# Branch and output projections of a hybrid decoder layer as three fp32r products of high and low parts

## What is computed

```python
o_a = nsa_attention(...)        # (1024, 512)
o_b = stick_breaking(...)       # (1024, 256)
o_c = swa_with_sinks(...)       # (1024, 256)
g = jax.nn.sigmoid(merge).reshape(B, S, 3, D)
y = g[:, :, 0] * (o_a @ w_branch_a) + g[:, :, 1] * (o_b @ w_branch_b) + g[:, :, 2] * (o_c @ w_branch_c)
return y @ w_out
...
x = x + g_a * hybrid_mixer(...)
h = rmsnorm(x, g_norm_moe[l]) * (1.0 + sc_m) + sh_m
x = x + g_m * grouped_moe(h, ...)
```

## Time and profile before

| | us |
|---|---|
| median of 3 runs | 2056.28 |
| lowest, highest | 2055.0, 2060.48 |
| the profiled execution | 2060.36 |
| its span, first to last instruction | 2058.6 |
| TensorE matmul busy | 1858.1 (90%) |
| DVE busy | 925.8 (45%) |
| ACT busy | 632.7 (31%) |
| mean granted TensorE clock | 0.951 of 2.4 GHz |

### The profile page before, as it was taken

One profiled execution on the slowest core, in us unless ns is written; L12 is line 12 of the kernel. 1 busy time (PEld: TensorE's weight loads), 2 busy tenths in 40 slices (PEclk: granted clock), 3 DMA queues, 4 the chain that ended last, 5 costly groups with the idle time before them and its releaser, 6 DMA issues.

```text
span 2058.6 us, 21698 instructions
## 1 busy us (share of the span) xinstructions
PE 1858.1 (90%) x7869; PEld 1202.3 (58%) x7869; DVE 925.8 (45%) x1505; ACT 632.7 (31%) x1115; POOL 243.7 (12%) x300
## 2 busy tenths in 40 slices
PE   2999999989898989989899888999984999999996
PEld 2554644555455555656556556444554777777875
DVE  5554313233333333334334344453336474759486
ACT  1321101323232323324234234210012353546363
POOL 3211230000000101001011011000001111111211
PEclk9999998999998999999999989999985999999998
DMA  9343321211011001001000040525233587879693
GB/s 341 124 148 119 81 54 25 62 42 42 28 34 33 30 21 36 26 21 36 21 21 16 11 128 6 209 92 214 103 110 84 173 286 200 289 244 348 192 367 94
DMA packets 121391, 232.33 MB, mean 113 GB/s; under 512 B 5832, under 2 KB 44816, under 8 KB 120240
## 3 DMA queue, kind: packets, MB, share of 16 engines
q1 hardware_dynamic: 113312, 203.14, 28.4%
q0 software_dynamic: 7984, 27.93, 6.0%
HBM read 196.44 MB, written 35.65 MB: 113 GB/s over the span
## 4 chain that ended last, share of the span: by engine, by line
PE 74%; DVE 16%; issue 4%; ACT 3%; DMA 1%; ACTq 0%; DVEq 0%; SPq 0%; POOL 0%; POOLq 0%
PE psum L1698 18%; PE psum L1524 9%; DVE arena_r L1403 9%; PE psum L1623 8%; PE psum L1684 7%; PE psum L1734 5%; PE psum L1759 5%; PE psum L1652 4%; PE psum L1544 3%; PE psum L1804 2%; PE psum L1805 2%; PE psum L1809 2%; ACT heads_r L932 1%; DVE negm L1206 1%; DVE kv L989 1%
## 5 line engine op out<-in xcount | busy, mean ns | idle before, releaser
L1698 PE MATMUL psum<-arena 128*128 128x512 f32 x768 | 387.9, 641 | 0.7 <-ACT arena L902 0.4
L1206 DVE TENSOR_REDUCE negm<-psum 128x1 f32<-128x640 f32 (+7 forms) x128 | 90.6, 707 | 431.1 <-PE psum L1625 431.1
L1684 PE MATMUL psum<-kv,arena 128*128 128x64 f32 x1464 | 197.4, 279 | 62.2 <-DVE arena L1190 36.7
L1684 PEld LDWEIGHTS psum<-kv,arena 128*128 128x128 f32 x1464 | 187.6, 200 | 69.9 <-issue 38.2
L1698 PEld LDWEIGHTS psum<-arena 128*128 128x128 f32 x768 | 144.8, 204 | 128.3 <-issue 127.8
L873 ACT ACTIVATE arena<-psum,negm 128x640 f32<-128x640 f32 (+7 forms) x128 | 89.6, 700 | 406.6 <-DVE negm L1206 406.5
L1524 PE MATMUL psum<-arena 128*128 128x512 f32 (+2 forms) x512 | 187.9, 520 | 0.0
L709 POOL TENSOR_SCALAR arena<-arena 128x128 f32<-128x128 f32 (+7 forms) x32 | 76.8, 2401 | 853.7 <-ACT arena L896 853.7
L1804 PE MATMUL psum<-heads_r,kv_r 128*128 128x512 f32 x384 | 151.0, 393 | 13.1 <-DVE kv_r L1409 13.1
L1623 PE MATMUL psum<-kv,heads 112*128 112x512 f32 (+7 forms) x384 | 147.5, 489 | 5.8 <-ACT arena L896 5.2
L1805 PE MATMUL psum<-heads_r,kv_r 128*128 128x512 f32 x384 | 150.8, 393 | 0.0
(11 more groups left out here) (356 smaller groups left out, 2454.7 us busy)
## 6 DMA issues: line engine op xcount, KB each, us to landing
arena<-in_w_exp_gate_dram SPq DMA_DIRECT2D x16, 2048.0 KB
arena<-in_w_exp_up_dram SPq DMA_DIRECT2D x16, 2048.0 KB, 13.1
arena<-in_w_exp_down_dram SPq DMA_DIRECT2D x16, 2048.0 KB, 10.6
arena<-in_w_ada_dram SPq DMA_DIRECT2D x7, 2048.0 KB, 15.2
arena<-in_w_in_dram SPq DMA_DIRECT2D x24, 512.0 KB, 4.1
z_dram<-arena SPq DMA_DIRECT2D x48, 256.0 KB, 2.0
arena<-z_dram SPq DMA_DIRECT2D x8, 1536.0 KB, 6.5
bc<-in_w_ada_dram SPq DMA_DIRECT2D x4, 2048.0 KB, 7.8
```

The source lines that it names most:

```text
L1684: mm = pe.matmul(psum[:, bank, c * HD:(c + 1) * HD], pt[:, j * P:(j + 1) * P], v, start=(j == 0), stop=(j == u["nb"] - 1))
L1698: mm = pe.matmul(GATE_BANK, gate_w[t % 3][:, k, :], hT[:, k, hf * BANK:(hf + 1) * BANK], start=(k == 0), stop=(k == NK - 1))
```

## The change

Both projections are made as the experts' are: high by high, high by low, low by high, in fp32r. The attention result is split in place (`o_hi` in the room of `hT`, `o_lo` over the float32 in `heads`) in the slots from 147 on; branch weights are loaded two groups ahead into a ring of two, and split; both halves of `w_out` are loaded behind z(1), and split in four pieces; `yT` is split tile by tile into rings of two; `x1` becomes a ring of two. The expert weights are loaded in another order. The diff, cut to what matters (index changes of `x1`, `oT` and semaphores left out):

```diff
+        SPLIT0 = FILL0 + 3 * N_GATE + 1
...
         def branch_w(m):
-            a = m % 4 * NK * P
-            return part_of(4 + m // 4, a, a + NK * P)...
+            a = m % 2 * NK * P
+            return part_of(0, a, a + NK * P)...
...
SP
-            for m in range(NK):
+            def load_branch(m):
                 for w, k0, k1 in ((w_branch_a, 0, 4), (w_branch_b, 4, 6), (w_branch_c, 6, 8)):
                     sp.dma_start(branch_w(m)[:, k0:k1, :], w...[:, :, m * P:(m + 1) * P]
-                                 ).then_inc(branch_in[m // 4], 16)
+                                 ).then_inc(branch_in[m % 2], 16)
...
             for i in range(2):
                 sp.wait_ge(z_out[i], 8 * N_GATE)
-            load(L_OUT)
+            load_branch(0)
+            load_branch(1)
...
             load_z(0)
             load_z(1)
-            load(L_OUT + 1)
-            for n in range(2):
-                sp.dma_start(xr[n], x2d[n * P:(n + 1) * P, :]).then_inc(xr_in[n], 16)
+            load_wout(0)
+            load_wout(1)
             for m in range(2, NK):
                 sp.wait_ge(mix_done, 6 * (m - 1))
                 load_z(m)
+                sp.wait_ge(mix_full, 6 * (m - 1))
+                load_branch(m)
...
             sp.wait_ge(mix_done, 3 * 2 * NK)
+            for n in range(2):
+                sp.dma_start(xr[n], x2d[n * P:(n + 1) * P, :]).then_inc(xr_in[n], 16)
+            load_expert(0, 0)
+            load_expert(0, 2)
...
+            sp.wait_ge(out_full, NT)
+            load_expert(0, 1)
             for i in range(3):
                 load_expert(1, i)
-            load_expert(0, 2)
...
POOL
-            pool.wait_ge(x1_out, 16 * NT)
+            for i in range(2):
+                pool.wait_ge(x1_out[i], 8 * NT)
...
ACT
+            def out_hi(n):
+                if n == 0:
+                    act.wait_ge(g_full, N_GATE)
+                for g in out_of[n]["groups"]:
+                    wait_evacuated(act, g)
+                act.activation(o_hi[:, n, :, :], o_raw[:, n, :, :], ACT.Copy).then_inc(o_hi_ok, 1)
+            def branch_weights_hi(m):
+                act.wait_ge(branch_in[m % 2], 16 * 3 * (m // 2 + 1))
+                if m >= 2:
+                    act.wait_ge(mix_full, 6 * (m - 1))
+                act.activation(branch_hi(m), branch_w(m), ACT.Copy).then_inc(bw_hi_ok, 1)
             for q, s in enumerate(slots):
...
+                if 0 <= q - SPLIT0 < NT - 1:
+                    out_hi(q - SPLIT0)
+                elif 0 <= q - SPLIT0 - (NT - 1) < 2:
+                    branch_weights_hi(q - SPLIT0 - (NT - 1))
+            out_hi(NT - 1)
             for m in range(NK):
                 act.wait_ge(z_in[m % 2], 16 * (m // 2 + 1))
                 act.activation(z_group(m), z_group(m), ACT.Sigmoid).then_inc(sig_ok, 1)
+                if m + 2 < NK:
+                    branch_weights_hi(m + 2)
+            act.wait_ge(mix_full, 3 * 2 * NK)
+            act.wait_ge(wout_in[0], wout_n[0])
+            act.activation(wout_chunk(wout_hi, 0), wout_chunk(wout_raw, 0), ACT.Copy).then_inc(wout_hi_ok, 1)
+            act.wait_ge(y_ok, 4 * NK)
             act.wait_ge(mix_done, 3 * 2 * NK)
+            mixed_hi(0)
+            act.wait_ge(wout_in[1], wout_n[1])
+            for c in range(1, 4):
+                act.activation(wout_chunk(wout_hi, c), wout_chunk(wout_raw, c), ACT.Copy).then_inc(wout_hi_ok, 1)
+            mixed_hi(1)
...
                     act.activation(xr[n % 2], x1[n % 2], ACT.Square, accum_out=st[:, SSX:SSX + 1]).then_inc(x1_sq, 1)
+                    if n + 2 < NT:
+                        mixed_hi(n + 2)
...
DVE
+                if 1 <= q - SPLIT0 < NT:
+                    out_lo(q - SPLIT0 - 1)
+                elif 0 <= q - SPLIT0 - NT < 2:
+                    branch_weights_lo(q - SPLIT0 - NT)
+            out_lo(NT - 1)
...
+                if r % 6 == 1 and 1 <= m < NK - 1:
+                    branch_weights_lo(m + 1)
...
             dve.wait_ge(y_ok, 4 * NK)
+            mixed_lo(0)
+            for c in range(4):
+                wout_rest(c)
+            mixed_lo(1)
...
+                    if n >= 2:
+                        dve.wait_ge(x1_out[n % 2], 16 * (n // 2))
...
+                    dve.tensor_tensor(x1[n % 2], x1[n % 2], xr[n % 2], ALU.add).then_inc(x1_ok, 1)
+                    if n + 2 < NT:
+                        mixed_lo(n + 2)
...
PE
-                if r % 24 == 0:
-                    pe.wait_ge(branch_in[m // 4], 16 * 12)
+                if r < 2:
+                    pe.wait_ge(o_hi_ok, 4 * (r + 1))
+                    pe.wait_ge(o_lo_ok, 4 * (r + 1))
+                if r % 6 == 0:
+                    pe.wait_ge(bw_hi_ok, m + 1)
...
                 for k in range(k0, k1):
-                    mm = pe.matmul(psum[:, 2 * (r % 4) + 1, :], branch_w(m)[:, k, :], oT[:, hf * 4:(hf + 1) * 4, k, :], ...)
+                    pe.matmul(bank, branch_hi(m)[:, k, :], o_hi[:, ns, k, :], start=(k == k0), stop=False)
+                    pe.matmul(bank, branch_hi(m)[:, k, :], o_lo[:, ns, k, :], start=False, stop=False)
+                if r % 6 == 0:
+                    pe.wait_ge(bw_lo_ok, m + 1)
+                for k in range(k0, k1):
+                    mm = pe.matmul(bank, branch_lo(m)[:, k, :], o_hi[:, ns, k, :], start=False, stop=(k == k1 - 1))
                 mm.then_inc(mix_full, 1)
...
+                    pe.wait_ge(y_hi_ok, n + 1)
+                    pe.wait_ge(y_lo_ok, n + 1)
```

More of the change, by code:

```diff
@@ L211, in slot_of @@
         def slot_of(i):
-            return HOME[i] if i < L_OUT else i - L_OUT
+            return HOME[i]
         slot_n = [[] for _ in range(5)]
@@ L243, in wait_used @@
                 eng.wait_ge(hid_full, 1)
-            elif i < L_OUT:
+            else:
                 eng.wait_ge(ada_ok, 4 + i - L_ADA2 + 1)
-            else:
-                eng.wait_ge(out_full, NT)
         prob = [tmp[:, i * T:(i + 1) * T] for i in range(2)]
@@ L571, in _ @@
             sp.wait_ge(mix_done, 3 * 2 * NK)
+            for n in range(2):
+                sp.dma_start(xr[n], x2d[n * P:(n + 1) * P, :]).then_inc(xr_in[n], 16)
+            load_expert(0, 0)
+            load_expert(0, 2)
+            for n in range(1, NT + 1):
+                if 2 <= n < NT:
+                    sp.wait_ge(xn2_ok, n - 1)
+                    sp.dma_start(xr[n % 2], x2d[n * P:(n + 1) * P, :]).then_inc(xr_in[n % 2], 16)
+                sp.wait_ge(xn2_ok, n)
+                sp.dma_start(xn_dram[(n - 1) * P:n * P, :], xn2).then_inc(xn2_out, 16)
+                sp.dma_start(out2d[(n - 1) * P:n * P, :], x1[(n - 1) % 2]).then_inc(x1_out[(n - 1) % 2], 16)
+            sp.wait_ge(out_full, NT)
+            load_expert(0, 1)
             for i in range(3):
                 load_expert(1, i)
-            load_expert(0, 2)
[L576 to L591, removed]
             sp.wait_ge(dest_ok, 1)
@@ L916, in _ @@
                         act.wait_ge(x1_rstd, n)
[L917 removed]
+                    act.activation(xr[n % 2], x1[n % 2], ACT.Square, accum_out=st[:, SSX:SSX + 1]).then_inc(x1_sq, 1)
+                    if n + 2 < NT:
+                        mixed_hi(n + 2)
                 if n:
@@ L937, in expert_tokens_hi @@
                                    ACT.Copy).then_inc(xs_hi_ok, 1)
-            act.wait_ge(x1_out, 16 * NT)
+            for i in range(2):
+                act.wait_ge(x1_out[i], 8 * NT)
+            act.wait_ge(xn2_out, 16 * NT)
+            act.wait_ge(y_lo_ok, NT)
             expert_weights_hi(0, None)
@@ L1300, in _ @@
                         dve.wait_ge(mod_rows_act, 1)
-                    own(dve.scalar_tensor_tensor(xn2, x1[:, n, :], stp[:, 1:2], a2_bc, ALU.mult, ALU.mult))
+                    own(dve.scalar_tensor_tensor(xn2, x1[n % 2], stp[:, 1:2], a2_bc, ALU.mult, ALU.mult))
                     dve.tensor_tensor(xn2, xn2, b2_bc, ALU.add).then_inc(xn2_ok, 1)
@@ L1756, in _ @@
                         pe.wait_ge(x1_ok, n - 1)
+                    pe.wait_ge(y_hi_ok, n + 1)
+                    pe.wait_ge(y_lo_ok, n + 1)
                     for h in range(2):
+                        w = wout_hi[h].rearrange("p (k n) -> p k n", k=NK)
                         for k in range(NK):
-                            mm = pe.matmul(psum[:, 2 * (n % 2) + h, :], yT[:, k, n * P:(n + 1) * P],
-                                           slot(slot_of(L_OUT + h))[:, k, :], start=(k == 0), stop=(k == NK - 1))
+                            if n == 0 and k % 4 == 0:
+                                pe.wait_ge(wout_hi_ok, 2 * h + k // 4 + 1)
+                            pe.matmul(psum[:, 2 * (n % 2) + h, :], y_hi[n % 2][:, k, :], w[:, k, :], start=(k == 0), stop=False)
+                            pe.matmul(psum[:, 2 * (n % 2) + h, :], y_lo[n % 2][:, k, :], w[:, k, :], start=False, stop=False)
+                    for h in range(2):
+                        w = wout_lo[h].rearrange("p (k n) -> p k n", k=NK)
```

(5 more changed lines are left out.)

63 lines of the change are left out of this document (50 added, 13 removed).

## The result

| median, us | before | changed | ratio, 95% interval |
|---|---|---|---|
| this pair | 2056.03 | 2078.19 | 1.0105 (1.0085 to 1.0124) |
| once more, beside another experiment | 2056.21 | 2079.41 | 1.0102 (1.0086 to 1.0119) |

The change makes the kernel slower by 22 us, where 16 us was forecast. The profiled executions lie closer: 2060.36 us before and 2076.89 us after, +16.5 us.

A forecast was written before the change was run, and what follows sets the result against it. TensorE was taken to bound the chain from 1285.55 to 1526.60 us. Slots 3.7, branch stage +35.2 and output stage -22.8 summed to +16.1 us: 2076.5 us profiled, median 2072.4, range 2057.9 to 2093.5.

The forecast's parts named there:

- The closed round: Branch stage, groups 1 to 6: sigmoids stand behind weight loads; 20.2 us a round, +35.2 us in place of -22.8.
- The gain of TensorE: Both stages: 10.88 us in place of 13.73 per group or tile, 22.8 us in either stage if TensorE stays bound.
- The attention slots: Three scan slots: a DVE subtraction delays the window maximum; 3 x 1.22 = 3.7 us, bounds 0 and 11.0 us.
- The bound of 7.3 us above the term: Attention slots: +7.3 us if all nine subtractions cost time, 9 x 1.22 = 11.0 us, where 3.7 was taken.
- Moved expert loads: Expert 0's up and all of expert 1 load from the output stage's end: zero; without cover 21 us.
- ring of x1: Output stage: the ring of two x1 tiles waits for stores one tile old; zero.
- SP's and POOL's waits: SP waits for nothing longer with stores ahead of the loads; POOL waits on two semaphores for one; zero.
- "not slower" rival: Both stages: loads run ahead, sigmoids find data early, TensorE bounds both; -41.9 us, 2014.4 us; chance 0.08.
- The half clock: Branch stage: idle time keeps TensorE at 1.2 GHz; 8 us more in rounds, 11.6 in tail, 2092 us; chance 0.12.
- The fit for a transfer: Round's loads: 2.0 us fixed, the rest at 436 GB/s, makes 6.8 us; sum 9.6 us lower; not adopted.
- the 8.4 of the rows: Round's loads: z 6.6 us and weights queued behind it 1.8 us, together 8.4 us; bounds 6.6 and 10.7.

The follow-up runs named there:

- both_orders: Changed kernel with ACT's copy after the sigmoid, SP's weight loads before z, and DVE's low part behind the fourth step; 2020.88 us, ratio 0.9819.
- both_orders_5: The same kernel as both_orders, run again in more rounds beside a repeat of both_and_slots; 2027.8 us, ratio 0.9856.
- experiment 3: The run of both_orders: ACT's and SP's orders both changed against the changed kernel, low part moved; 2020.88 us, ratio 0.9819.
- both_and_slots: both_orders with DVE's nine attention-slot subtractions moved to slots without the stick-breaking scan; 2012.75 us, ratio 0.9775; repeated, 2013.01 us, ratio 0.9792.
- slots_only: Changed kernel with only DVE's nine subtractions moved to slots without the stick-breaking scan; 2071.66 us, ratio 1.0073.
- output_only: Changed kernel with its branch stage back in fp32 and no splits there or in the slots, weights still loaded in the ring; 2036.46 us, ratio 0.9896.

## Why the forecast was right, and where it was off

- **The closed round: right.** Forecast: sigmoids about 20 us apart from the second on, each behind a weight copy that waits for its load, and a stage end at 148.5 us from its start. Measured: 19.8 us, as said, and 148.3 us from TensorE's first branch matmul (1289.28) to 1437.59. Of the round's terms the loads were 8.3 us in the mean instead of 8.4, and DVE and ACT 11.5 instead of 11.8 with the hand-offs. Some of the fit is luck: five rounds took 99.1 us instead of 101.0, and the end of the stage from DVE's start of group 6 19.0 us instead of 17.8. TensorE's idle time in a round was 5.8 to 9.2 us, not about 9, since its bursts begin at half clock. The runs show the round as cause, not only as pattern: taking the load out of the sigmoids' way on ACT gives 25 us, issuing it earlier gives 44 us, and both 50 to 57 us, at unchanged work. In the profiles, from z(0) to the modulation rows, the gains are 23.9, 43.0 and 56.3 us.
- **The gain of TensorE: right.** 10.88 us per group (both_orders: 92 us for the stage) and 13.52 us per tile. The output stage gained 21.0 us instead of 22.8, since the modulation rows took 5.46 us where they took 3.84. TensorE begins them at half clock (the mean of 1436 to 1440 is 0.74), which the forecast had only in the branch stage. In both_orders they take 3.84 us again, in both_orders_5 5.47 us, behind the same pause of 2.07 us, so this too changes between executions.
- **The attention slots: the mechanism was right, the size off.** The forecast had "3 x 1.22 = 3.7 us" and took the clock as no part of it. The pauses are longer by 3 x 1.14 = 3.4 us, and at equal clock the stretch by 3.7 us, so the term itself is right. The place of the subtractions is worth 7.7 us in the medians of the changed kernel (8 and 15 us in the two pairs with both orders mended), and its profiles are 4.2 and 8.3 us over the kernel before in that stretch. The 4 us above the term are most of the gap between the forecast 16 and the measured 22 us. The bound of 7.3 us above the term, which the forecast had for the other six subtractions, covered it by luck.
- **Moved expert loads, ring of x1, SP's and POOL's waits: zero, right.** The part behind the output stage is 530.9 us long, and was 532.0.
- **The rivals.** The time of the "not slower" rival, 2014.4 us, is what the kernel reaches once the order is mended and the subtractions are moved: 2012.75 and 2013.01 us. It was put down to a misreading of the order, and its own condition is what experiment 3 establishes. The half clock did not stay: the burst shown reaches 1.00 before its end, as "by that each burst starts slow but not each stays slow" had it; the Trainium skill, page "TensorE: Matmul & The Clock Gate", section "HAM oscillation", describes this pattern, and the stretches of the round shown above agree. The mean clock over the span is 0.941 and 0.937 in two profiles of the changed kernel, and 0.951 in that of the kernel before.
- **The fit for a transfer.** By the Trainium skill, page "DMA: Bandwidth & Descriptors", section "Anatomy of one DMA", whose fit is for another issuing path, z and weights would take 6.8 us (estimate). The trace has 7.9 to 9.4 us to the start of the copy, in the mean 8.3, so the 8.4 of the rows was the better choice.

## What to carry to other kernels

When a load moves inside a loop, look for what stands behind its wait on the engine that takes it, not only for its bytes: here 1 us of copying, in front of a sigmoid that had its data, turned a double buffer into a closed round. The stage came out 35 us longer than before the change, and 56 us longer than the same work in the other order. Two rules decide it: issue a load as soon as the buffer's reader is done, and put the work that waits for it behind the work that does not. And extra work belongs in slots where the next instruction of that engine waits anyway, since where it delays TensorE its price can be more than its length (here 7.7 us for 3.7).

## What the runs showed of the hardware that I had not expected

- The granted clock of one stretch differs between executions of one kernel: both_and_slots has 0.87 and 91.0 us, its repeat 0.92 and 87.3 us, the changed kernel 0.87 and 94.7 us, then 0.80 and 98.8 us. TensorE's busy time there is 75.1 us at 0.92 and 85.1 us at 0.80, for the same 444 instructions.
- A pause of 1.25 us before the same four matmuls is followed by 1.98 us for them in slots_only (1236.02, mean clock 1.00 from 1235 to 1240) and by 3.67 us in the kernel before (1237.87, 0.72 from 1237 to 1243).
- The kernel before loads 4 MB of branch weights and 2 MB of `w_out` in that stretch (DMA share 0.25). output_only loads 1 MB there (0.05), has the same work on all engines, and takes 90.52 us where the kernel before takes 90.54: these loads cost the attention slots nothing.
